# First attention: both halves' mean squares from high and low parts, into the score bank

## The reference

```
def rms_norm(x, g):
    xf = x.astype(jnp.float32)
    y = xf * lax.rsqrt(jnp.mean(xf * xf, axis=-1, keepdims=True) + EPS)
    return (y * g.astype(jnp.float32)).astype(x.dtype)
...
    q = rms_norm(q.reshape(b, s, N_Q_HEADS, HEAD_DIM), q_norm_g)
    k = rms_norm(k.reshape(b, s, N_KV_HEADS, HEAD_DIM), k_norm_g)
    v = v.reshape(b, s, N_KV_HEADS, HEAD_DIM)
    o = sliding_window_attention(q, k, v, sinks) * jax.nn.silu(z_a)
```

## Time and profile before

| | before |
|---|---|
| median of 3 runs | 2440.23 us (2437.32 to 2440.41) |
| profiled execution, its own time | 2440.13 us |
| its span, first to last instruction | 2438.4 us |
| PE busy | 2413.1 us, 99% |
| DVE, ACT, POOL busy | 64%, 45%, 56% |
| mean granted TensorE clock | 0.999 |

### The profile page before, as it was taken

How to read it: one execution, slowest core, us unless ns; L and a number is a source line. 1 busy time by engine, 2 the same in 40 slices (tenths; PEclk the granted TensorE clock), 3 DMA queues, 4 the chain that set the end, 5 groups by cost and what they waited for, 6 DMA issues and landing times. The chain is left out here.

```text
span 2438.4 us, 35805 instructions
## 1 busy us (share of the span) xinstructions
PE 2413.1 (99%) x11528; PEld 1996.0 (82%) x11528; DVE 1568.0 (64%) x2281; ACT 1099.5 (45%) x2030; POOL 1370.0 (56%) x1221
## 2 busy tenths in 40 slices
PE   9999999999999999999999999999999999999999
PEld 7788888888888878888888888777888888888887
DVE  8655552344677785435666666756868777777886
ACT  6333233301666661126777777832433333344442
POOL 4788887443455554443222222254289888666683
PEclk9999999999999999999999999999999999999999
DMA  4222223589210015332111111431133333487652
GB/s 144 67 80 68 61 76 109 181 282 328 76 35 26 26 35 189 125 111 70 61 61 60 60 60 61 157 120 52 63 106 124 116 116 113 149 274 222 187 181 87
DMA packets 128949, 275.65 MB, mean 113 GB/s; under 512 B 14144, under 2 KB 14528, under 8 KB 128848
## 3 DMA queue, kind: packets, MB, share of 16 engines
q1 hardware_dynamic: 83712, 155.75, 20.3%
q10 hardware_dynamic: 45136, 118.67, 13.5%
HBM read 206.41 MB, written 67.96 MB: 113 GB/s over the span
## 5 line engine op out<-in xcount | busy, mean ns | idle before, releaser
L683 POOL TENSOR_SCALAR whi<-raw 128x512 fp32r<-128x512 f32 x190 | 136.4, 718 | 335.1 <-PE bank L903 170.5
L685 POOL TENSOR_TENSOR wlo<-raw,whi 128x512 fp32r<-128x512 f32 x190 | 266.5, 1403 | 15.9
L698 POOL TENSOR_TENSOR wlo<-a,whi 128x512 fp32r<-128x512 f32 x114 | 163.6, 1435 | 41.4 <-ACT whi L1905 41.2
L903 PE MATMUL bank<-b_lo,whi 128*128 128x512 f32 x448 | 175.3, 391 | 0.0
L903 PE MATMUL bank<-a_hi,whi 128*128 128x512 f32 x400 | 158.2, 396 | 2.4 <-DVE a_lo L2819 1.4
L966 PE MATMUL bank<-b_hi,whi 128*128 128x512 f32 x384 | 156.9, 409 | 0.2 <-ACT f_raw L1684 0.2
L966 PE MATMUL bank<-b_hi,wlo 128*128 128x512 f32 x384 | 150.7, 392 | 0.0
L966 PE MATMUL bank<-b_lo,whi 128*128 128x512 f32 x384 | 150.2, 391 | 0.0
L811 POOL COPY fc<-fc 128x128 f32<-128x128 f32 x96 | 28.0, 292 | 192.9 <-DVE mx L2749 192.9
L1905 ACT ACTIVATE whi<-a 128x512 fp32r<-128x512 f32 x114 | 70.7, 627 | 133.7 <-PE bank L1246 51.6
L903 PE MATMUL bank<-b_hi,whi 128*128 128x512 f32 x320 | 125.3, 392 | 1.0 <-ACT up_g L2305 0.6
(11 more groups left out here) (793 smaller groups left out, 7870.8 us busy)
## 6 DMA issues: line engine op xcount, KB each, us to landing
raw<-in_w SPq DMA_DIRECT2D x202, 256.0 KB, 2.6
a<-in_pairs SPq DMA_DIRECT2D x152, 256.0 KB, 2.7
fc<-c_scr ACTq DMA_DIRECT2D x32, 512.0 KB, 3.6
wd_scr<-wd SPq DMA_DIRECT2D x55, 256.0 KB, 5.4
wd<-in_down SPq DMA_DIRECT2D x44, 256.0 KB, 4.9
xs_scr<-made ACTq DMA_DIRECT2D x40, 256.0 KB, 2.6
h_scr<-up_y ACTq DMA_DIRECT2D x13, 512.0 KB, 2.6
raw<-wd_scr SPq DMA_DIRECT2D x26, 256.0 KB, 3.0
```

The costliest lines, as they stand in the source:

```text
L683: nc.gpsimd.tensor_scalar(hi, src, 1.0, 1.0, ALU.mult, ALU.mult).then_inc(w_hi, 1)
L685: nc.gpsimd.tensor_tensor(lo, src, hi.bitcast(F32), ALU.subtract).then_inc(w_lo, 1)
L698: nc.gpsimd.tensor_tensor(ring[1][pos], src[:].rearrange("p (k c) -> p k c", c=P), ring[0][pos].bitcast(F32), ALU.subtract).then_inc(ww_lo, 1)
L903: last = nc.tensor.matmul(psum_ap, ws[w][:, k, :], a[:, kt, hs(h)], start=(first and i == 0 and j == 0), stop=(final and i == n - 1 and j ...
```

## The change

The mean square becomes two float32r matmuls for a half, `head_mean` by the high part of the square and by its low part. `head_mean` is now float32r and is made by one more POOL instruction at the start. ACT's Square writes the high part. DVE computes the square again in float32 and subtracts the high part: two new instructions for a half (`square_lo`). PE now waits for these, through the semaphore `q_n`. In the pairs both halves' mean squares stand together behind the third k step of `fill(1, 0)` and go into the two halves of `score[0]`, and ACT takes one logarithm and one root of 1024 columns. ACT's wait for `og` (the previous pair's gated output) moves ahead of query(0), since `sq_hi` lies where `s_z` does. The early tiles keep their logarithms and roots by halves.

```diff
-            def mean_square(n, h, dst, square):
-
-                pe.wait_ge(sw.q_sq, n * 2 + (h + 1))
-                nc.tensor.matmul(dst, head_mean[:], square[:, hs(h)], start=True, stop=True).then_inc(sw.q_ms, 1)
+            def mean_square(n, h, dst, square_hi, square_lo):
+
+                pe.wait_ge(sw.q_n, n * 5 + (2 * h + 2))
+                nc.tensor.matmul(dst, head_mean[:], square_hi[:, hs(h)], start=True, stop=False)
+                nc.tensor.matmul(dst, head_mean[:], square_lo[:, hs(h)], start=False, stop=True).then_inc(sw.q_ms, 1)
...
                 scores(2)
                 fill(0, 1, range(2))
-                pe.wait_ge(sw.lo, st + 1)
-                mean_square(n, 0, flip[:], s_sq)
                 values(0)
...
-                fill(1, 0, range(2))
+                fill(1, 0, range(3))
                 pe.wait_ge(sw.exp, st * 4 + 12)
-                mean_square(n, 1, score[0][:, 0:HALF], s_sq)
-                fill(1, 0, range(2, 3))
-                pe.wait_ge(sw.q_std, n * 2 + 1)
+                for h in range(2):
+                    mean_square(n, h, score[0][:, hs(h)], sq_hi, sq_lo)
+                pe.wait_ge(sw.lo, st + 1)
                 flip_p(2)
...
+            def whole_log_mean(n, square):
+
+                act.wait_ge(sw.q_ms, n * 2 + 2)
+                nc.scalar.activation(square[:], score[0][:], ACT.Ln, bias=eps_rms[:]).then_inc(sw.q_std, 2)
+
+            def whole_root(n, square):
+
+                act.wait_ge(sw.q_std, n * 2 + 2)
+                settle()
+                nc.scalar.activation(square[:], square[:], ACT.Exp, scale=-0.5).then_inc(sw.q_rstd, 2)
...
                 act.wait_ge(sw.q_lo, it * 4 + (2 * pp + 6))
+                act.wait_ge(sw.og, it * 8 + 4 * pp)
                 query(0)
-                log_mean(flip[:], n, 0, s_sq)
                 fold(0)
...
                 expo(3)
-                log_mean(score[0][:, 0:HALF], n, 1, s_sq)
+                whole_log_mean(n, s_sq)
                 high(2)
-                one_over_root(n, s_sq)
+                whole_root(n, s_sq)
...
+            def square_lo(n, h, t, raw, square, hi, lo):
+
+                dve.wait_ge(tile_out[h], t + 1)
+                v.tensor_tensor(square[:, hs(h)], raw[:, hs(h)], raw[:, hs(h)], ALU.mult).then_inc(sw.q_n, 1)
+                dve.wait_ge(sw.q_n, n * 5 + (2 * h + 1))
+                dve.wait_ge(sw.q_sq, n * 2 + (h + 1))
+                v.tensor_tensor(lo[:, hs(h)], square[:, hs(h)], hi[:, hs(h)].bitcast(F32), ALU.subtract).then_inc(sw.q_n, 1)
...
                 maxima(2)
+                query_lo(0)
                 add(0)
                 low(1)
                 normalise(2)
                 maxima(3)
+                query_lo(1)
                 add(1)
...
             for c, (gain, hi, lo) in enumerate(((C_KG, s_k[0], sk_lo[0]), (C_KG, s_k[1], sk_lo[1]), (C_QG, s_q, None))):
+                for h in range(2):
+                    square_lo(c, h, U_SWA + c, early[2 * c], early[2 * c + 1], early_hi[c], early_lo[c])
                 normed(c, gain, early[2 * c], early[2 * c + 1])
                 if c < 2:
                     down_sums(KT + 1 + c)
```

More of the change, by code:

```diff
@@ L252, in build @@
         mask_r = fixed("mask_r", [P, 3 * P], F32R)
-        head_mean = fixed("head_mean", [P, P], F32)
+        head_mean = fixed("head_mean", [P, P], F32R)
         feat_mean = fixed("feat_mean", [P, P], F32)
@@ L282, in build @@
         early_raw = overlay(b_lo_at + 16 * 1024, *((f"early_raw{b}", [P, HALF], F32) for b in range(2)))
-        (mask_f,) = overlay(b_hi_at, ("mask_f", [P, 3 * P], F32))
+        mask_f, head_mean_f = overlay(b_hi_at, ("mask_f", [P, 3 * P], F32), ("head_mean_f", [P, P], F32))
         def psum(name, n):
@@ L313, in build @@
         early = [s_o[:, j, :] for j in range(KT)]
+        sq_hi, sq_lo = overlay(over_at + 24 * 1024, ("sq_hi", [P, S], F32R), ("sq_lo", [P, S], F32R))
+        early_hi, early_lo = (sq_hi, sp_lo, sq_hi), [b_hi[:, 2 * c + 1, :] for c in range(3)]
         v_flips = [[score[1][:, h * HALF:(h + 1) * HALF] for h in range(2)], [flip[:], bank[1][:]]]
@@ L655, in _ @@
             nc.gpsimd.memset(mask_f[:], 0.0).then_inc(const_made, 1)
-            nc.gpsimd.memset(head_mean[:], 0.0).then_inc(const_made, 1)
+            nc.gpsimd.memset(head_mean_f[:], 0.0).then_inc(const_made, 1)
             pool.wait_ge(const_made, 6)
@@ L667, in _ @@
             for h in range(2):
-                nc.gpsimd.memset(head_mean[h * DH:(h + 1) * DH, h * DH:(h + 1) * DH], 1.0 / DH).then_inc(const_made, 1)
+                nc.gpsimd.memset(head_mean_f[h * DH:(h + 1) * DH, h * DH:(h + 1) * DH], 1.0 / DH).then_inc(const_made, 1)
             pool.wait_ge(const_made, 12)
@@ L671, in _ @@
             nc.gpsimd.tensor_scalar(mask_r[:], mask_f[:], 1.0, 1.0, ALU.mult, ALU.mult).then_inc(const_made, 1)
+            nc.gpsimd.tensor_scalar(head_mean[:], head_mean_f[:], 1.0, 1.0, ALU.mult, ALU.mult).then_inc(const_made, 1)
             settle = settler(pool)
@@ L1298, in _ @@
                     tile(j * 2 + (U_MIX + 2 + c), j * 2 + (U_MIX + 2 + c), c, b_hi, b_lo)
-            pe.wait_ge(const_made, 14)
+            pe.wait_ge(const_made, 15)
             pe.wait_ge(prepared, 6)
@@ L1308, in _ @@
                             pe.wait_ge(sw.q_std, 2 * (c - 1))
-                        mean_square(c - 1, h, score[0][:, hs(h)], early[2 * c - 1])
+                        mean_square(c - 1, h, score[0][:, hs(h)], early_hi[c - 1], early_lo[c - 1])
             for t in range(2):
@@ L1553, in v_hi, with raw_and_square @@
                                      src.rearrange("p (b h d) -> p b h d", h=2, d=DH), ACT.Copy).then_inc(at.v_hi, 1)
-            def raw_and_square(src, t, n, h, raw, square):
+            def raw_and_square(src, t, h, raw, square_hi):
                 act.wait_ge(tile_done[h], t + 1)
@@ L1559, in raw_and_square @@
                 act.wait_ge(tile_out[h], t + 1)
-                nc.scalar.activation(square[:, hs(h)], raw[:, hs(h)], ACT.Square).then_inc(sw.q_sq, 1)
+                nc.scalar.activation(square_hi[:, hs(h)], raw[:, hs(h)], ACT.Square).then_inc(sw.q_sq, 1)
             def log_mean(src, n, h, square):
@@ L1573, in normed_hi @@
             def normed_hi(dst, n, raw):
-                act.wait_ge(sw.q_n, n + 1)
+                act.wait_ge(sw.q_n, n * 5 + 5)
                 for hh, rows in enumerate(head_rows):
@@ L1620, in query @@
                 def query(h):
-                    raw_and_square(bank[0], it * 4 + u0, n, h, s_raw, s_sq)
+                    raw_and_square(bank[0], it * 4 + u0, h, s_raw, sq_hi)
                 def gate_a(h):
@@ L1961, in _ @@
                 nc.scalar.activation(cv_v[:, hs(h)], third_bank[h], ACT.Silu).then_inc(tile_out[h], 1)
-            act.wait_ge(const_made, 14)
+            act.wait_ge(const_made, 15)
             act.wait_ge(w_lo, 3 * 2 + 2)
@@ L2118, in early_square @@
                 for h in range(2):
-                    raw_and_square(bank[h], U_SWA + c, c, h, early[2 * c], early[2 * c + 1])
+                    raw_and_square(bank[h], U_SWA + c, h, early[2 * c], early_hi[c])
             def early_root(c):
@@ L2628, in low, with query_lo @@
                     window_low(it, pp, s)
+                def query_lo(h):
+                    square_lo(n, h, it * 4 + u0, s_raw, s_sq, sq_hi, sq_lo)
                 def add(s):
```

1 line of the change is left out of this document (removed).

## The result

The changed kernel takes 2466.68 us (median of 4 runs, 2465.43 to 2468.95), the kernel before 2438.82 (4 runs, 2437.32 to 2440.41). The ratio is 1.011, with a 95% interval of 1.0098 to 1.0123: slower by 1.1%, where 2475 was forecast. The profiled execution took 2465.43 us, with a span of 2463.7, which is 25.3 more than before's 2438.4.

What follows compares the result with a forecast made beforehand. PE was taken to bound the kernel, so its saved passes and its waits count in full. 2440.1 + 21.0 (early tiles) + 4.2 (clock) + 10.2 (pairs) = 2475.5 us, range 2453 to 2485.

Steps and rivals of the forecast that it cites:

- Early tiles: Three early mean squares, n = 0, 1 and 2: PE waits for DVE's square_lo, +21.0 us, PE's saving of 2.4 included.
- n = 1: Second early mean square: square_lo stands behind normed_lo of n = 0, which needs ACT's high parts; +8.0 us.
- n = 2: Third early mean square: square_lo stands behind normed_lo of n = 1, with a POOL split beside it; +7.7 us.
- n = 0: First early mean square: square_lo stands behind down_sums and takes turns with POOL splits; +5.3 us, bounds +2.4 and +5.3.
- The clock: Matmuls at half rate after PE's idle time behind tiles 2 and 3: +4.2 us, bounds 0 and +5.0.
- 2 x 2.1: The clock's sum: two slow stretches, behind tiles 2 and 3, each losing 2.1 us, between 1.8 and 2.5.
- The pairs: Seven pairs, each +1.45 us from late half 1 low parts and late high(2): +10.2, bounds -5.6 and +17.9.
- square at 691.0, subtraction at 692.15: Second pair: square_lo of half 1 meets POOL's splits, wlo included, so PE ends half 1 at 692.7.
- +0.6, instead of the -0.8 of the removed passes: A pair's mean squares: PE waits for half 1's low part, so the pair is 0.6 us longer there.
- the wait at the low values: PE's wait at values(2) in a pair: high(2) comes later behind the whole logarithm, +0.85 us.
- the pairs gain: Rival: early tiles lose, but half 1's low parts are in time in the pairs; 2459.7 us, chance 0.36 (gaining or even).
- The middle value for an unknown turn: Pairs: DVE and POOL turns put at +1.45 us a pair, between -0.8 and +2.55; forecast case chance 0.42.

Runs made afterwards that it cites:

- e_fill: The changed kernel with useless matmuls filling PE's waits ahead of the early mean squares; 2459.61 us, ratio to before 1.0089.
- e_early: The changed kernel with the early tiles' square_lo moved ahead in DVE's order, n = 0 ahead of the last down_sums; 2437.86 us, ratio to before 0.9993.
- e_order: As e_early, but the low parts of n = 0 stay behind down_sums, as in the changed kernel; 2444.31 us, ratio to before 1.0016.
- e_hi: The changed kernel without the square's low part: one matmul for a half, no square_lo on DVE (computation incomplete); 2429.97 us, ratio to before 0.9958.
- e_mid: e_early with the pairs' logarithm by halves and high(2) between the two; 2435.09 us, ratio to before 0.9980.

## Why the prediction was right, and where not

**Early tiles, +21.0 forecast.** Right in mechanism, and in size for n = 1 and n = 2. Everything over before is 24.65, the clock's share 6.04 by e_fill, so 18.6 is left. By tile, from PE's coming to the first product behind the mean squares, less the 1.72 of before: n = 0 is 5.86 - 1.72 = +4.1 (596.29 to 602.15; +5.3 forecast, with two long turns of POOL, of which one came: the four took 0.68, 0.98, 1.76 and 0.98), n = 1 is 10.2 - 1.72 = +8.5 (614.20 to 624.40; +8.0 forecast), n = 2 +8.2 (+7.7 forecast). The three make 20.8. The tiles behind them are longer by 3.84 together (12.05, 12.84 and 11.74 from first to last product, 10.93 each before), and that is the whole of the 24.65. The lower clock is in both parts, some 0.5 of it in the mean squares of each tile: 3.84 + 1.6 = 5.4 by the rows, 6.04 by e_fill. Without it the three tiles are 3.6, 8.0 and 7.7, 19.2 by the rows, so the term was 2 too large, nearly all of it at n = 0. That place in the order is the cause, and not the new work, is shown by e_early, where the same instructions cost no wait; e_order shows it for n = 0 alone.

**The clock, +4.2 forecast, bounds 0 and +5.0.** The mechanism was right, the size too small and outside its bounds: 6.04 by e_fill. The step that failed is "2 x 2.1": there were three slow stretches and not two, of 1.7, 2.4 and 1.3 by the rows. The wait of n = 0, two idle times under 2 us each, also brought the clock down, which no term of the sum had. That early tiles and clock together come so near (25.2 forecast, 24.65 measured) is luck: the waits were forecast 1.8 to 2.4 too high, and the clock 1.2 to 1.8 too low.

**The pairs, +10.2 forecast, -0.55 measured.** Here a step failed. The prediction put `square_lo` of half 1 behind POOL's `wlo`, "square at 691.0, subtraction at 692.15", and so had "+0.6, instead of the -0.8 of the removed passes". In the trace the square went ahead of `wlo` and PE had no wait at the mean squares. The other step, the wait at the low values behind the whole logarithm, came, with 0.56 for the forecast 0.85. Over seven pairs: -5.6 for the passes and 0.56 x 7 = +3.9 for that wait is -1.7, and measured is -0.55. The remaining 1.1 us are the short wait at `values(1)`, 0.18 in six pairs. The prediction had `low(1)` end later and `sp_lo(1)` need it, but put no cost on it. e_hi, without DVE's added instructions, is without this wait. The rival "the pairs gain" was right about the mean squares, but it had forgotten the wait at the low values that the forecast itself had named. With it, and all else as forecast, 2440.1 + 21.0 + 4.2 - 1.7 gives 2463.6, against 2465.43 for the profiled execution.

**The middle value for an unknown turn.** The rows of before had neg_max(3) and `wlo` 0.08 apart. A turn that is decided by so little can fall either way, and a loss for every pair was put on it with the largest single chance. Multiplied by seven it was the largest error of the sum.

## What to carry to other kernels

On an engine that works in order, the cost of a new instruction is first of all what stands ahead of it: here the same twelve instructions cost 27 us or nothing, by whether they wait behind work that itself waits for a later event. Where PE sets the time, price its idle time together with the slow matmuls behind it, for short idle times too. Waits that the view does not list count too, so compare distances of starts between kernels. And when two small operations of a side engine become one large one, look for an urgent small one queued behind it: the single logarithm of 1024 columns saved ACT time that nobody waited for, and taking it by halves again gave PE back 0.36 of the 0.56 us of each pair.

## What the runs showed of the hardware beyond what was expected

- **Short idle times bring the clock down too.** Idle times of 1.87 and 1.75 us, with one half's mean square (two matmuls) between them (e_order), were followed by products 0.43 apart from 602.19 to 605.60. The Trainium skill ("TensorE: Matmul & The Clock Gate", Why this matters for your kernels) says that an idle gap between bursts of matmuls brings half rate back, and the trace agrees in that. But the gaps that it warns of are longer than either of these, and there the measurement decides.
- **The slow stretch is not longer for a longer idle time.** In the changed kernel five slow products followed 1.98 + 1.97 us, nine followed 7.72, and four followed 7.43.
- **The granted clock shows it here and did not at the start.** The windows over the slow stretches have 0.89 and 0.88, where the first matmuls of the kernel ran slow at a row of 1.00.
- **The turns between DVE and POOL stretch either side.** `wlo`, 1.3 us when alone, was recorded with 1.77 when DVE's square had begun 0.07 ahead of it, and the subtraction behind it with 1.58 for 0.69.
- **A short wait of PE leaves no idle time on record.** A product of 512 columns is recorded with 0.39 us and the next starts 0.23 later. Waits of 0.18 to 0.22 us at `values(1)`, and in e_mid at the low values and the gate, show in no view of waits, only in the distances of starts.
